# Two-stage token fetch, regrouped scan and gating products, and half-block norms in a two-block transformer kernel

## The reference

```python
# first block
proj = rms_norm(x, g) @ w_in                       # xa, zu, zv, two gates
bu = einsum('gpc,lbgc->lbgp', b_bar, xa)           # both directions
_, states = associative_scan(_linear_recurrence, (a, bu), axis=0, reverse=reverse)
y = einsum('gcp,lbgp->lbgc', c, states).real       # + D skip, gelu, GLU
sv = einsum('hts,bnshd->bnthd', w_s, layer_norm(gelu(zv))) + bias
yb = gelu(zu) * sv                                 # spatial gate
k, v = memn @ w_k, memn @ w_v
# second block, per layer
m = (g_na * y_na + g_sw * y_sw) @ w_out            # y_*: two attentions of x @ w_in
x = layer_norm_2(ALPHA * x + m, ln1_g, ln1_b)
f = swiglu_2(x, ...) if layer == 0 else moe_swiglu(x, ...)
x = layer_norm_2(ALPHA * x + f, ln2_g, ln2_b)
# mixture of experts: 8 experts, each token goes to 2
y = y + combine[:, e:e + 1] * swiglu_2(xt, w_gate[e], w_up[e], w_down[e])
```

## Time and profile before

| | us |
|---|---|
| median of 3 runs | 2141.72 |
| lowest and highest | 2138.93, 2142.01 |
| the profiled execution | 2138.8 |
| its span | 2137.0 |
| busy in the span: PE, DVE, ACT | 2097.1, 1544.6, 1177.6 |
| granted clock of PE, mean | 0.993 |

### The profile page before, as it was taken

One profiled execution on the slowest core, in us unless ns is written; L12 is line 12 of the kernel. 1 busy time (PEld: TensorE's weight loads), 2 busy tenths in 40 slices (PEclk: granted clock), 3 DMA queues, 4 the chain that ended last, 5 costly groups with the idle time before them and its releaser, 6 DMA issues.

```text
span 2137.0 us, 33255 instructions
## 1 busy us (share of the span) xinstructions
PE 2097.1 (98%) x12608; PEld 1837.3 (86%) x12608; DVE 1544.6 (72%) x1829; ACT 1177.6 (55%) x1204; POOL 13.3 (1%) x24
## 2 busy tenths in 40 slices
PE   9999999999999899999999999999999999999997
PEld 8888899999898899989887888888888888888885
DVE  8776356555555644454658989898998989899897
ACT  4302245434346333434717777776777777777774
POOL 0000000000000000000000000000000000000000
PEclk9999999999999999999999999999999999999999
DMA  8343443545552455555246989898998989899893
GB/s 327 140 143 133 172 156 127 193 180 188 228 176 97 158 180 178 191 223 178 100 157 264 379 346 362 342 365 347 364 369 344 363 335 370 346 366 360 349 359 154
DMA packets 76182, 540.03 MB, mean 253 GB/s; under 512 B 9136, under 2 KB 9280, under 8 KB 11952
## 3 DMA queue, kind: packets, MB, share of 16 engines
q1 hardware_dynamic: 71856, 522.22, 63.5%
q0 software_dynamic: 2080, 10.40, 1.3%
q10 hardware_dynamic: 2144, 5.93, 0.7%
HBM read 537.47 MB, written 1.05 MB: 252 GB/s over the span
## 4 chain that ended last, share of the span: by engine, by line
PE 88%; DVE 8%; issue 2%; ACT 2%; DVEq 1%; ACTq 0%
PE psum L1353 14%; PE psum L939 12%; PE psum L1330 10%; PE psum L1333 10%; PE psum L1334 10%; PE psum L779 6%; PE psum L952 5%; PE psum L751 5%; PE psum L715 4%; PE psum L702 2%; DVE scan_t L2268 2%; DVE big L2274 1%; DVE scan_t L2271 1%; PE psum L764 1%; PE psum L1285 1%
## 5 line engine op out<-in xcount | busy, mean ns | idle before, releaser
L2495 DVE TENSOR_TENSOR w_l<-ring,w_h 128x2048 fp32r<-128x2048 f32 x336 | 768.7, 2290 | 104.5 <-ACT w_h L1534 98.7
L1534 ACT ACTIVATE w_h<-ring 128x2048 fp32r<-128x2048 f32 x336 | 646.1, 1923 | 131.8 <-PE psum L1330 92.5
L1330 PE MATMUL psum<-w_h,xe_h 128*128 128x512 f32 x896 | 359.4, 401 | 0.9 <-DVE w_l L2495 0.9
L1334 PE MATMUL psum<-w_h,xe_l 128*128 128x512 f32 x896 | 349.8, 390 | 0.0
L1333 PE MATMUL psum<-w_l,xe_h 128*128 128x512 f32 x896 | 349.8, 390 | 0.0
L2087 DVE TENSOR_TENSOR wf_l<-ring,wf_h 128x2048 fp32r<-128x2048 f32 x66 | 151.1, 2291 | 135.6 <-ACT wf_h L1525 135.6
L2058 DVE TENSOR_TENSOR wp_l<-ring,wp_h 128x2048 fp32r<-128x2048 f32 x52 | 119.0, 2290 | 116.3 <-ACT wp_h L1548 116.3
L1330 PEld LDWEIGHTS psum<-w_h,xe_h 128*128 128x128 f32 x896 | 168.2, 188 | 37.1 <-DVE w_l L2495 3.9
L1334 PEld LDWEIGHTS psum<-w_h,xe_l 128*128 128x128 f32 x896 | 168.2, 188 | 36.2
L939 PE MATMUL psum<-xf_h,wf_h 128*128 128x256 f32 x688 | 195.7, 285 | 1.7 <-DVE xf_l L2095 1.7
L1333 PEld LDWEIGHTS psum<-w_l,xe_h 128*128 128x128 f32 x896 | 168.7, 188 | 31.9
(11 more groups left out here) (442 smaller groups left out, 3635.0 us busy)
## 6 DMA issues: line engine op xcount, KB each, us to landing
ring<-in_stream SPq DMA_DIRECT2D x497, 1024.0 KB, 6.1
big<-in_bc POOLq DMA_DIRECT2D x11, 512.0 KB, 7.3
big<-in_na_bias POOLq DMA_DIRECT2D x2, 2048.0 KB, 9.0
h<-in_x SPq DMA_DIRECT2D x2, 512.0 KB, 4.2
big<-in_mem ACTq DMA_DIRECT2D x1, 1024.0 KB, 12.8
big<-in_s_c ACTq DMA_DIRECT2D x1, 1024.0 KB, 17.3
r_k<-in_sgu_ln ACTq DMA_DIRECT2D x1, 1024.0 KB, 21.8
out_dram<-ysum ACTq DMA_DIRECT2D x2, 512.0 KB, 2.7
```

Of the source, the lines that this page charges most:

```text
L1330: first = nc.tensor.matmul(out, xe_h[:, k, :], wh[:, i, :], start=(k == 0), stop=False)
L1334: last = nc.tensor.matmul(out, xe_l[:, k, :], wh[:, i, :], start=False, stop=(k == KD - 1))
L1534: nc.scalar.activation(high, src, ACT.Copy).then_inc(w_high, 1)
L2495: V.tensor_tensor(low, src, high.bitcast(F32), ALU.subtract).then_inc(w_split, 1)
```

## The change

There are five edits.

1. `bu` runs without the `zu` product in it; `zu` 0 comes after `kmat`.
2. `sgu` moves between `v` 1 and `v` 2. The turned states have four sets of buffers instead of two, laid over `xT`, `r_zv` and `sguT`, and the waits for `y` 0 and 1 fall. DVE's turning now waits for `gb` 3 and `sgu` 3.
3. `out` 2 and `last` become one: `last` 0 and 1 now are 512 columns (512 to 1023) of one block. The chunk `w_out` 3 is split into a buffer of the feed-forward (`LENT`), so its copy no longer waits for a product.
4. A norm's last operation is cut into two halves of 512 columns (`xn_half`, `xn_ready`), and PE's transposes take each half when it is there. In the mixer the transposes of block 1 stand in the middle of the second run of 24 products on block 0 instead of behind it.
5. From the second pass on the tokens are fetched in two stages: `pick_rows` (step 12) uses `pick` as weights and `h` as the moving operand, 8 products of 512 columns, ACT copies the rows (`move_rows`, between the copies of chunks 39 and 40), and `turn_rows` (step 13, behind the gate and up products) transposes them, 8 of 128 columns. The first fetch keeps the old form.

```diff
 BORROWED = {SPLIT_AT[("k8", f"w_in_{m}", 2)]: (m + 1) * FF_STEPS for m in range(2)}
+LENT = [SPLIT_AT[("k8", f"w_out_{m}", 3)] for m in range(2)]
...
-                    [big[:, 9216:10240], memT[:, 4:8, :].rearrange("p k t -> p (k t)")]]
+                    [xT[:, 0:4, :].rearrange("p k t -> p (k t)"), xT[:, 4:8, :].rearrange("p k t -> p (k t)")],
+                    [big[:, 9216:10240], r_zv[:, 0:1024]],
+                    [sguT[:, :, :].rearrange("p k m -> p (k m)"), r_zv[:, 1024:2048]]]
...
+            def normed_transposes(u0, b, n):
+
+                for half in range(2):
+                    pe.wait_ge(xn_ready if half else xn_half, n + 1)
...
             for u0 in range(0, BLK // 2, 4):
-                if u0 == 8:
-                    form_a(("zu", 0), ("k8", "w_in", 6), xT)
...
-                for b in range(TB):
-                    pe.wait_ge(acc_free, 2 * m + b + 1)
-                    pe.wait_ge(xn_ready, 1 + 4 * m + b)
-                    block_transposes(f"t_in{m}", h, b)
...
+                for b, i in ((0, 0), (0, 1), (1, 0), (1, 1)):
+                    if b == 0:
+                        open_unit(pe, (f"projb{m}", i))
+                    last = split_b_block((f"projb{m}", i), ("k8", f"w_in_{m}", i), b, b,
+                                         turned=f"t_in{m}" if i == 0 else None,
+                                         halfway=second_block if (b, i) == (0, 1) else None)
...
-                    close_unit(split_b_block((f"last{m}", b), ("k8", f"w_out_{m}", 3), b, 0), (f"last{m}", b))
+                    for i in range(2):
+                        last = split_b_block((f"last{m}", b), ("k8", f"w_out_{m}", 2 + i), b, i)
+                    close_unit(last, (f"last{m}", b))
...
+            def pick_rows():
+
+                for b in range(TB):
+                    for part in (h_h, h_l):
+                        for c in range(2):
+                            last = nc.tensor.matmul(psum[:, 6 + c, :], pick[:, b, :], part[:, b, c * 512:(c + 1) * 512],
...
+            def turn_rows(n):
+
+                pe.wait_ge(rows_moved, n)
+                for k in range(KD):
+                    last = nc.tensor.transpose(psum[:, 6 + k // 4, (k % 4) * P:(k % 4 + 1) * P],
+                                               picked_rows[:, k * P:(k + 1) * P], ident[:, :])
+                last.then_inc(gathered, 1)
...
-                        gather(1)
+                        pick_rows()
                     if s == LAST:
+                        if not last_pass:
+                            turn_rows(p + 1)
                         transpose_h(p, s - 1)
...
+            def move_rows(n):
+                act.wait_ge(rows_picked, n)
+                nc.scalar.activation(picked_rows.rearrange("p (c d) -> p c d", c=2), psum[:, 6:8, :],
+                                     ACT.Copy).then_inc(rows_moved, 1)
...
-                V.scalar_tensor_tensor(x[:, b, :], x[:, b, :], rstd[:, b:b + 1], b_, ALU.mult, ALU.add
-                                       ).then_inc(xn_ready, 1)
+                for half, ready in enumerate((xn_half, xn_ready)):
+                    cols = slice(512 * half, 512 * half + 512)
+                    V.scalar_tensor_tensor(x[:, b, cols], x[:, b, cols], rstd[:, b:b + 1], b_[:, cols],
+                                           ALU.mult, ALU.add).then_inc(ready, 1)
...
-            evacuated(dve, ("v", 3))
+            evacuated(dve, ("gb", 3))
+            take_unit(dve, ("sgu", 3))
             for q in range(1, 4):
-                if q >= 2:
-                    take_unit(dve, ("y", q - 2))
...
-                    hs = h[:, b, 768:1024]
-                    free_unit(V.scalar_tensor_tensor(hs, hs, ALPHA, bank(u)[:, 0:256], ALU.mult, ALU.add), u)
+                    hs = h[:, b, 512:1024]
+                    free_unit(V.scalar_tensor_tensor(hs, hs, ALPHA, bank(u), ALU.mult, ALU.add), u)
```

More of the change, by code:

```diff
@@ L145, in split_plan @@
         out += [(("k8", f"w_in_{m}", i), unit) for i, unit in enumerate(units)]
-        out += [(("k8", f"w_out_{m}", i), (f"out{m}", i) if i < 3 else (f"last{m}", TB - 1)) for i in range(4)]
+        out += [(("k8", f"w_out_{m}", i), (f"out{m}", i) if i < 2 else (f"last{m}", TB - 1)) for i in range(4)]
     return out
@@ L167, in plan_units @@
     u.append(("xa", 1))
-    u += [("bu", i) for i in range(8)] + [("zu", 0)] + [("bu", i) for i in range(8, BLK // 2)]
+    add("bu", BLK // 2)
     add("kmat", 1)
-    u += [("zu", i) for i in range(1, 4)]
+    add("zu", 4)
     add("ga", 4)
@@ L695, in block_transposes @@
                     close_unit(last, u)
+            def normed_transposes(u0, b, n):
+                for half in range(2):
+                    pe.wait_ge(xn_ready if half else xn_half, n + 1)
+                    u = (u0, 2 * b + half)
+                    open_unit(pe, u)
+                    for k in range(4):
+                        last = nc.tensor.transpose(bank(u)[:, k * P:(k + 1) * P],
+                                                   h[:, b, (4 * half + k) * P:(4 * half + k + 1) * P], ident[:, :])
+                    close_unit(last, u)
             def form_a(unit, chunk, act_T):
@@ L768, in split_half, with split_b_block @@
                 close_unit(last, unit)
-            def split_b_block(unit, chunk, b, at, x_h=xf_h, x_l=xf_l, turned=None, filled=None):
+            def split_b_block(unit, chunk, b, at, x_h=xf_h, x_l=xf_l, turned=None, filled=None, halfway=None):
                 wh, wl = split_chunk(chunk)
                 for k in range(KD):
+                    if halfway is not None and k == KD // 2:
+                        halfway()
                     if turned is not None and k % 4 == 0:
@@ L1078, in _ @@
             close_unit(last, ("kmat", 0))
-            for i in range(1, 4):
+            for i in range(4):
                 form_a(("zu", i), ("k8", "w_in", 6 + i), xT)
@@ L1087, in _ @@
                 form_a(("k", i), ("k8", "w_k", i), memT)
-            for i in range(4):
+            for i in range(2):
                 form_b(("v", i), ("k8", "w_v", i), memT)
@@ L1101, in _ @@
                 close_unit(last, ("sgu", u))
+            for i in range(2, 4):
+                form_b(("v", i), ("k8", "w_v", i), memT)
             evacuated(pe, ("kmat", 0))
@@ L1545, in wp_part @@
                     act.wait_ge(u_full, BORROWED[n])
-                elif n >= 2:
+                elif n >= 2 and n not in LENT:
                     take_unit(act, SPLIT[n - 2][1])
@@ L1664, in _ @@
             act.dma_start(big[:, 8192:9216], a["sgu_bias"].to_broadcast([P, D])).then_inc(loads["sbias"], 16)
-            for i in range(1, 4):
+            act.wait_ge(cneg_ready, 1)
+            for i in range(4):
                 move_zu(i)
@@ L1862, in one_expert @@
                         move_oe(p)
+                    if (part, s) == ("gate", LAST) and not last_pass:
+                        move_rows(p + 1)
                     if part == "up":
@@ L2408, in _ @@
                 block_rstd(b)
-                V.scalar_tensor_tensor(h[:, b, :], h[:, b, :], rstd[:, one], bc[:, 3, :], ALU.mult, ALU.add
-                                       ).then_inc(xn_ready, 1)
+                for half, ready in enumerate((xn_half, xn_ready)):
+                    cols = slice(512 * half, 512 * half + 512)
+                    V.scalar_tensor_tensor(h[:, b, cols], h[:, b, cols], rstd[:, one], bc[:, 3, cols],
+                                           ALU.mult, ALU.add).then_inc(ready, 1)
             dve.wait_ge(xn_ready, 2)
```

74 lines of the change are left out of this document (38 added, 36 removed).

## The result

The changed kernel takes 2122.89 us (median of four executions, 2122.21 to 2123.45), the kernel before 2141.8 (median of four, 2138.93 to 2142.01): a ratio of 0.9915, 95% interval 0.9897 to 0.9932. The profiled execution of the changed kernel took 2122.61 us, with a span of 2120.8; against that of before it gained 16.2 us.

What follows compares the result with a forecast made beforehand. PE, with work for 98% of the span, was taken as the bound. 4.6 + 1.3 + 1.2 + 1.5 + 2.0 + 0.4 = 11.0 us off the profiled 2138.8 gave 2127.8; with the median 2.9 higher, forecast 2130.5, range 2124 to 2137.5.

Steps and rivals of the forecast that it cites:

- second mixer's end: Behind the second mixer: DVE's norm comes earlier and PE's wait of 0.42 us goes, 0.4 us gained.
- token fetch: Seven later passes: 0.8 us less each, minus 0.15 lag of the split chain; 4.6 us gained, bounds 5.7 and 0.
- The price of a transpose: Token fetch: PE pays the 0.11 us interval; rival, chance 0.05: it is held 271 ns, kernel at 2139.6.
- the cover of the row copy: Token fetch: ACT's row copy lies beside step 13's products, costed at nothing; 1.02 us a pass without that cover.
- Scan: The scan ends 6.4 us earlier, so states are turned and the gate multiplied sooner; `pb` 1.3 us earlier.
- First mixer's start: Block 1's transposes moved ahead of 12 products: 1.2 us gained; block 0 brings nothing.
- its end: First mixer's end: merged output products and halved norm start the feed-forward earlier, 2.0 us gained, bounds 1.2 and 2.6.
- second mixer's start: Half norms and earlier transposes: block 0 gains 0.35 us, both blocks together 1.5 us.
- the last rival: More than forecast: no lag in passes, no bank waits in the scan, warm clock at 553; 2126.5, chance 0.07.
- The split chain: Rival in the passes: DVE and ACT set the length and take the fetch's gain; 2135.3, chance 0.14.
- ACT didn't miss its turn: Rival in the passes: the row copy makes a weight copy a whole chunk late; 2150, chance 0.04.
- The clock fell in no new place: Rival: low clock at second mixer's start (1.5 us) and longer at the feed-forward's start (1.9); 2134, chance 0.09.

Runs made afterwards that it cites:

- e11: The kernel before, unchanged, run again to profile an execution of the upper group: 2141.85 us.
- e9: The kernel before with only `bu` in one run, `zu` 0 behind it: 164.06 us from first `bu` product to `pb`, before 163.50.
- e7: The changed kernel with the eight transposes of each later token fetch made twice: 2130.44 us, one execution.
- e8: The changed kernel with ACT's copy of the picked rows made twice: 2123.18 us, one execution.
- e1: The kernel before with only the two-stage token fetch in the seven later passes: 2131.87 us, ratio 0.9971.
- e2: The kernel before with only the scan edits (`bu` in one run, `sgu` between `v` pieces, four sets of states): 2137.26 us, ratio 0.9991.
- e10: The kernel before with only `sgu` moved and four sets of states: 161.93 us from first `bu` product to `pb`, before 163.50.
- e13: The changed kernel with `zu` 0 back between the halves of `bu`: 2122.85 us, ratio to before 0.992.
- e5: The kernel before with one more filler product behind the first block's transposes at the second mixer's end: 2137.56 us, ratio 0.9989.
- e3: The kernel before with only the norm halves and the earlier transposes of block 1: 2133.53 us, ratio 0.9971.
- e4: The kernel before with only the last two output products merged and `w_out` 3 in a lent buffer: 2135.42 us, ratio 0.998.

## Why the prediction missed

It forecast 2130.5 and measured was 2122.9: 7.6 us, of which 5.2 lie between the sum of 11.0 and the 16.2 us of the profiled executions, and 2.4 in the step from there to the median. Three steps failed: the price of the wait at the second mixer's end (2.0 us), the lag charged to the token fetch, with small gains left out of it (2.1), and the offset carried over to the median (2.4).

- **From the profiled execution to the median: 2.7 us carried over, 0.3 measured.** I took before's offset of 2.9 us for something outside the kernel and carried it over (2127.8 and 2.9 are 2130.7; the forecast of 2130.5 has 2.7 of it). It belonged to the kernel: two of the three executions I had were of the upper group, whose slow stretch e11 shows at the very place that edits 3 and 4 mend. Three executions of which two lie together and one 2.8 us below were the hint.
- **Second mixer's end, 0.4 forecast, 2.38 measured.** The mechanism, DVE's norm ahead of PE, was right; its price was read from the wait alone. The 1.77 us more that the following transposes and fillers take at half clock stood in the trace of before. They aren't in every execution: e9 shows the same wait without them, so a part of the 2.38 us depends on which execution of before was profiled. I priced the clock at 553 and at the feed-forward's start, and not here, where a window of the trace says 0.89.
- **Token fetch, 4.6 forecast, 6.72 measured.** Of 0.65 a pass it became 0.98. The 0.84 us by counted intervals came as worked out (0.8). The lag of 0.15 was not there: I had the split chain 1.03 us later and PE 0.9, and both came 0.8 later. And about 0.15 came on top, as the lags that shrank. The price of a transpose, the cover of the row copy and the bound of 5.7 (the last too low) are the parts that e7, e8 and e1 tested.
- **Scan, 1.3 forecast, 1.51 measured: right size, wrong reason.** I said that the earlier scan lets the states be turned and the gate be multiplied sooner. The gate's product did stop being last. Of the two waits for banks one came in the changed kernel's profile, 0.7 us where I said 0.8 for both; e2 and e9 show both, 1.1 us. But without the earlier scan the gain is as large (e10, e13): the size came out right by luck.
- **First mixer's start 1.40 (1.2), its end 1.89 (2.0), second mixer's start 1.44 (1.5): right.** At the first mixer's end the feed-forward starts 2.25 us sooner after `first_b`, 0.3 more than worked out, and its 192 products take 0.36 us longer than before (25.55 instead of 25.19), within what they take in other executions of before's form (25.08 to 25.69); so 1.89 is in part a balance of the two. The chains from half a norm to transposes, low part and first product came as followed, and the lent buffer held nothing up.
- **Rivals.** Two of their sums are slightly off and decide nothing: 7 x 2.1 is 14.7, and the three gains of the last rival add to 3.8, so 2126.7. The split chain took nothing, PE pays the interval of a transpose, ACT didn't miss its turn. The clock fell in no new place; the error was to look for that and not for the place where it would stop falling.

## To carry to other kernels

A short wait of the product engine can have two prices, its length and, in some executions, the clock of what follows (here 0, 1.7 or 4.6 us behind a wait of 0.42); read the granted clock behind each wait that an edit removes, and compare the same instructions' interval elsewhere. Executions of one kernel that form two groups are a reading of the kernel: ask which stretch differs before carrying an offset over. Where an engine must wait anyway, products without use, written to a bank that is overwritten next, gave 3.6 us here; and of an edit with two halves, try each alone, since one may pay for the other.

## Not expected of the hardware

That a wait of 0.42 us, between transposes, fillers and products of 8 columns, is followed by some 4 us of instructions at 1.2 GHz in some executions, by some 10 us in others of the same kernel, and by none in e9; and that 0.86 us of filler ahead of the wait ends both slow forms. Whether the filler's own activity or the missing wait does it, e5 alone can't tell; e3 and e4 removed the wait without adding a product, and had the full clock too. What decides between the three outcomes was not tried.
